# Masks a level ahead, one projection moved, norm sums two fills later, and weight slabs in 8 KB rows

## Time and profile before

| | |
|---|---|
| median of three runs | 1447.91 us |
| profiled execution: its own time | 1451.15 us |
| its span, first to last instruction | 1449.3 us |
| mean granted clock of TensorE | 0.926 |
| busy share PE / DVE / ACT / POOL | 80% / 51% / 34% / 26% |
| DMA: bytes, mean rate | 377.58 MB, 261 GB/s |
| chain that ended last | PE 48%, DMA 24%, DVE 18%, ACT 7% |

### The profile page before, as it was taken

How to read it: one execution, slowest core, us unless ns; L and a number is a source line. 1 busy time by engine, 2 the same in 40 slices (tenths; PEclk the granted TensorE clock), 3 DMA queues, 4 the chain that set the end, 5 groups by cost and what they waited for, 6 DMA issues and landing times.

```text
span 1449.3 us, 15054 instructions
## 1 busy us (share of the span) xinstructions
PE 1160.8 (80%) x5592; PEld 674.0 (47%) x5592; DVE 745.7 (51%) x1811; ACT 487.0 (34%) x1283; POOL 370.6 (26%) x285
## 2 busy tenths in 40 slices
PE   6799885868867676666677766679988998999997
PEld 2588653422422231111122221134866887889883
DVE  5113468758769965465444445530455656652102
ACT  1022124443433433344333333321576543112201
POOL 0868202243434444433343433300000000000000
PEclk9998998999988999998998999989998999999999
DMA  9953605789999999999999999915422131114230
GB/s 365 304 218 146 246 1 201 308 326 416 412 414 420 410 412 397 421 421 407 423 386 404 396 401 422 421 65 176 174 68 107 59 117 60 60 59 160 73 116 29
DMA packets 92164, 377.58 MB, mean 261 GB/s; under 512 B 6355, under 2 KB 9596, under 8 KB 59260
## 3 DMA queue, kind: packets, MB, share of 16 engines
q0 software_dynamic: 36864, 268.45, 45.3%
q1 hardware_dynamic: 54560, 106.13, 20.4%
q10 hardware_dynamic: 668, 2.04, 0.4%
HBM read 375.54 MB, written 1.06 MB: 260 GB/s over the span
## 4 chain that ended last, share of the span: by engine, by line
PE 48%; DMA 24%; DVE 18%; ACT 7%; issue 2%; POOL 1%; SPq 1%; DVEq 0%; POOLq 0%; ACTq 0%
PE ps L87 48%; DMA AR<-in_puv,idx 20%; DVE AR L87 8%; DVE RT L87 3%; ACT L87 2%; DVE tok L87 2%; DMA mixT<-scr 1%; ACT av L87 1%; DMA W<-in_w_mod 1%; DVE acc L87 1%; DVE rowb L87 1%; DVE mixT L87 1%; ACT acc L87 1%; POOL AR L87 1%; ACT rowb L87 1%
## 5 line engine op out<-in xcount | busy, mean ns | idle before, releaser
L87 PE MATMUL ps<-AR,acc 128*64 128x512 f32 x960 | 371.2, 689 | 184.3 <-ACT acc L87 183.1
L87 POOL DMA_INDIRECT AR<-in_puv,idx x256 | 278.1, 1086 | 502.1 <-PE ps L87 394.0
L87 PE MATMUL ps<-hT,W 128*128 128x256 f32 (+2 forms) x1504 | 324.6, 374 | 2.6 <-ACT hT L87 2.5
L87 PEld LDWEIGHTS ps<-hT,W 128*128 128x128 f32 (+1 forms) x1504 | 270.4, 195 | 54.8 <-issue 15.9
L87 PEld LDWEIGHTS ps<-AR,acc 128*64 128x64 f32 x960 | 90.2, 149 | 439.3 <-ACT acc L87 356.8
L87 DVE CUSTOM_DVE_ANT_0 AR<-AR,mixT 128x1024 f32<-128x1024 f32 x128 | 156.7, 1227 | 157.0 <-DMA AR<-in_puv,idx 156.8
L87 DVE CUSTOM_DVE_ANT_0 AR<-AR,tok 128x1024 f32<-128x1024 f32 x128 | 153.1, 1219 | 66.3 <-DMA AR<-in_puv,idx 66.2
L87 ACT ACTIVATE av<-av 128x1 f32<-128x1 f32 x256 | 51.3, 200 | 311.5 <-DVE av L87 311.3
L87 ACT ACT_TABLE_LOAD x105 | 134.7, 1283 | 11.4 <-DVE tok L87 9.5
L87 PE MATMUL ps<-W,hT 128*128 128x512 f32 (+3 forms) x288 | 97.8, 497 | 0.8 <-ACT hT L87 0.8
L87 ACT ACTIVATE acc<-fold,av 128x64 f32<-128x64 f32 x240 | 83.5, 348 | 7.8
(11 more groups left out here) (230 smaller groups left out, 1087.5 us busy)
## 6 DMA issues: line engine op xcount, KB each, us to landing
W<-in_w_in SPq DMA_DIRECT2D x25, 2048.0 KB, 8.4
W<-in_w_mod SPq DMA_DIRECT2D x12, 2048.0 KB, 17.4
W<-in_w_out SPq DMA_DIRECT2D x2, 2048.0 KB, 10.3
W<-in_wq SPq DMA_DIRECT2D x2, 2048.0 KB, 10.2
AR<-in_puv,idx POOLq DMA_INDIRECT x256, 11.3
W<-in_wba SPq DMA_DIRECT2D x2, 2048.0 KB, 7.7
W<-in_wbb SPq DMA_DIRECT2D x2, 2048.0 KB, 8.6
W<-in_wo SPq DMA_DIRECT2D x2, 2048.0 KB, 7.7
```

Source lines behind the costliest of these rows:

```text
L87: ins = f(*args, **kw)
```

## The change

Four edits. In `load_w` a slab is read by two DMAs of 1 MB each, and the host lays every weight matrix out so that the eight pieces of a partition stand side by side in device memory: each DMA has 128 rows of 8 KB (of four times the slab's width where it is narrower than 512; then the rows in SBUF stay apart). The l2 norm's steps stand 0, 2, 3, 4 and 5 fills behind instead of 0 to 4. `za_step(3)` is issued after the first group's mask and difference, in front of its transposes. The masks of level 1 wait only for the difference, and those of level l + 1 are issued in level l, behind its first products, each after the last product that read its `CT[:, n]`.

```diff
             if i < len(plan):
                 src, a, n = plan[i]
-                landed[i] = SP.dma(nc.sync.dma_start, wsem[i % NSLOT], W[:, i % NSLOT, :, 0:n],
-                                   src[:, a:a + n].rearrange("(k p) n -> p k n", p=P), after=after)
+                for k in (0, 4):
+                    landed[i] = SP.dma(nc.sync.dma_start, wsem[i % NSLOT], W[:, i % NSLOT, k:k + 4, 0:n],
+                                       src[:, 8 * a + k * n:8 * a + (k + 4) * n].rearrange("p (k n) -> p k n", k=4), after=after)
...
-            for n, f in enumerate((l2_square, l2_sums, l2_diag, l2_spread, l2_scale)):
+            for n, f in ((0, l2_square), (2, l2_sums), (3, l2_diag), (4, l2_spread), (5, l2_scale)):
                 if s - n in L2:
                     f(L2.index(s - n))
...
-                za_step(n)
+                if n < 3:
+                    za_step(n)
...
             t = V(tt_, tt4, ident.unsqueeze(1).to_broadcast([P, 4, P]), CT[:, n], SUB,
                   after=[t, t_turn["q", 0], t_turn["q", 1]])
+            if n == 0:
+                za_step(3)
...
+        def masked(l, n, after):
+            return V(tt_, CT[:, n], MTv[n // 2][:, 4 * (n % 2):4 * (n % 2) + 4, :], mask(l), MUL, after=after)
+
+        t_cm = [masked(1, n, state[n][:1]) for n in range(4)]
+        t_xp = [None] * 4
         for l in range(1, 7):
             xs = []
             for n in range(4):
-                a, g4 = n // 2, n % 2
-                t = V(tt_, CT[:, n], MTv[a][:, 4 * g4:4 * g4 + 4, :], mask(l), MUL, after=state[n])
-                b, src, p_ = product(l, CT[:, n], Tm[:, 4 * n:4 * n + 4, :], [t] + state[n])
+                b, src, p_ = product(l, CT[:, n], Tm[:, 4 * n:4 * n + 4, :], [t_cm[n]] + state[n])
+                t_xp[n] = p_
...
+            if l < 6:
+                t_cm = [masked(l + 1, n, [t_xp[n]]) for n in range(4)]
             run_filler()
...
+    def slabs(w, cuts=None):
+
+        cuts = cuts or range(0, w.shape[1] + 1, 512)
+        return np.concatenate([w[:, lo:hi].reshape(8, P, hi - lo).transpose(1, 0, 2).reshape(P, -1)
+                               for lo, hi in itertools.pairwise(cuts)], axis=1)
```

More of the change, by code:

```diff
@@ L1 @@
+import itertools
 import math
@@ L1924 @@
     w_out = np.concatenate([pair(w_out[0:512]), w_out[512:]])
+    def slabs(w, cuts=None):
+        cuts = cuts or range(0, w.shape[1] + 1, 512)
+        return np.concatenate([w[:, lo:hi].reshape(8, P, hi - lo).transpose(1, 0, 2).reshape(P, -1)
+                               for lo, hi in itertools.pairwise(cuts)], axis=1)
     ins = [("x", a["x"][0]), ("cst", k), ("oh", onehot), ("pc", pc), ("cmpw", cmpw), ("keysT", keysT),
-           ("rel", a["rel_table"]), ("rows", rows), ("ab", ab), ("w_mod", a["w_mod"][0]), ("w_in", w_in),
-           ("w_out", w_out), ("wq", a["peer_wq"][0]), ("puv", np.concatenate([a["peer_u"][0], a["peer_v"][0]], axis=1)),
-           ("w_in2", a["w_in_2"][0]), ("wba", a["w_branch_a_2"][0]), ("wbb", a["w_branch_b_2"][0]),
-           ("wo2", a["w_out_2"][0])]
+           ("rel", a["rel_table"]), ("rows", rows), ("ab", ab), ("w_mod", slabs(a["w_mod"][0])),
+           ("w_in", slabs(w_in, (0, 512, 1024, 1304, 1816, 2328, 2840))),
+           ("w_out", slabs(w_out)), ("wq", slabs(a["peer_wq"][0])),
+           ("puv", np.concatenate([a["peer_u"][0], a["peer_v"][0]], axis=1)),
+           ("w_in2", slabs(a["w_in_2"][0], (*range(0, 8193, 512), 8208, 8720, 9232, 9744, 10256))),
+           ("wba", slabs(a["w_branch_a_2"][0])), ("wbb", slabs(a["w_branch_b_2"][0])), ("wo2", slabs(a["w_out_2"][0]))]
     nc = bacc.Bacc("TRN2", target_bir_lowering=False, num_devices=1)
```

## The result

The changed kernel took 1430.93 us (median of four runs, 1426.61 to 1434.69) against 1448.8 of the kernel before (four runs): a ratio of 0.9881 [0.9856, 0.9907]. Run again beside others it took 1430.29, a ratio of 0.9901 [0.9865, 0.9937]. Forecast were 1424 and the range 1411 to 1438. The time lies in that range, and about 18 us were gained instead of 24.

A forecast was written before the change was run, and what follows sets the result against it. The bound changes by stage: DMA gathers from 553 to 950 us, PE from 1128.2 to 1161.8. Gains 2.5 + 2 + 9.5 + 3 + 7 = 24 us, from the median 1447.9 to 1424; range 1411 to 1438.

The forecast's parts named there:

- rival A: Whole kernel: all gains come as summed, 1424 us, own range 1413 to 1433; chance 0.62.
- the start: Kernel start: X, K and `scr` come 5 us later, covered by PE's wait for `mixT`; `flip_bias` starts 2.5 us earlier.
- za: Last za projection: first transposes follow it at once, removing PE's 4.04 us idle; gain 3 us, bounds 1.5 and 4.
- the masks: Levels: masks fall into V's idle, so PE's five waits before levels 2 to 6 go; gain 7.0 us, bounds 5 and 7.5.
- the norm sums: Conv blocks: sums two fills behind spare PE the wait for the square; gain 9.5 us, bounds 3 and 13.
- rival C: Conv blocks: PE waits for diagonals instead, lower clock stays; norm change gains 3, not 9.5: 1430.5 us; chance 0.13.
- Gathers and the projection behind them: Gather stage: six slabs sharing DMA engines with the gathers give time back; gain 2 us, bounds 0 and 3.6.
- one more sum and one more spread: Norm steps after the seven columns, where PE is the bound: these fall there and cost 1.7 us together.
- The cover of 6.79 us: Start: PE's earlier wait for `mixT`, 6.79 us, which was to hide the later q projection.
- if PE also loses its half clock in these 6.18 us: Start: upper bound if `flip_bias`, then 6.18 us, no longer runs at half clock; gain 4 to 5 us.
- Rival D: Slab loads: long direct rows come slowly, slower than before, about 1510 or 1465 us; chance 0.07.
- Its second case: Slab loads: only w_mod's rows run at half rate because of their pitch, +5.6 us per slab; about 1465 us.

## Why the prediction was right, and where its sum was off

The forecast was faster, by the mechanisms of rival A, and faster it is: the start, za and the masks by the mechanisms that were forecast, the norm sums only in part. The time itself, 1430.9, is the number of rival C (1430.5). Its reason, PE waiting for diagonals, is not what came (0.4 us), but a part of its outcome is: waits that stay, and the lower clock behind them. That the number agrees is chance: C had 3 for the norm sums and all other terms as summed, and the ledger has 5.2, and terms that differ from the sum by up to 4.5. The terms, in us of the profiled pair: the start to `mixT` and what follows, forecast 2.5, measured 3.5 by the projection behind `flip_bias`. Gathers and the projection behind them, forecast 2, measured -2.5 (what was 3.5 ahead at 62 us is 0.98 at the first conv copy). Norm sums, forecast 9.5, measured 5.2. za, forecast 3, measured 2.5. Masks, forecast 7, measured 6.4 in the levels and 1.4 behind the last one: 7.8. In all 24 and 16.5.

**The failed step** is the norm sums' price. The column spacings were forecast as 5.6, 6.8, 4.7, 7.7, 4.7, 8.4 and 4.7, and came as 5.5, 6.6, 4.7, 7.5, 4.7, 11.7 and 4.7. All but one were right. The one is the column with the scale, and behind the seven another one with a scale took 9.6 us where 4.1 stood before (11.2 to 11.3 in four other kernels with the same norm steps, whose conv stages take 128.6 to 128.9 us); "one more sum and one more spread" and a wait "for a diagonal" had been priced there at 4.1 together, and 5.5 were lost. The prediction looked for the next wait at the diagonal and bounded it by a wait in each pair; rival C was the same thought. It was the PSUM bank of the spread, held until the scale, which the change also moves and which the prediction counted only as V's time. The two waits of 2.5 us stood in the list of PE's waits of the kernel before, for the very stretch of the earlier trace rows, and had not been read: the prediction put ACT's two idles of 3.47 us down to the square, and so expected them to go with it. With the scale moved, the stage gains 12.1 us (132.64 to 120.52), so the forecast size was available, though not by the edit that was forecast.

**The gather stage** was missed in the execution that the ledger uses, and met on average. From PE's first transposes of `rowb` (`K,rowb`) near 247 us to PE's transposes behind the last gather, the five kernels with 2 KB rows took 699.5 to 702.7 us (mean 700.9); seven others with 8 KB rows 695.6 to 699.3, and the changed kernel's own profile 701.7. The mean of all eight is 698.2: a gain of 2.7 where 2 had been said. The profile that the ledger uses is the worst of the eight, so the miss of 4.5 in this term says little of the edit. What differs from one execution to the next in that stage stays open, and no run tests whether the price of a row is what the average gains.

**What was right by its steps.** X lands 4.0 us later (V starts on it at 15.34 for 11.35), K 5.8 (16.9 us from issue to landing for 11.1) and `scr` 6.3; they had been forecast as 5, from one row for one row. The cover of 6.79 us held with little to spare, since the q projection starts 6.0 later and not 4.2: `flip_bias` starts 0.9 us earlier instead of 2.5. The bound "if PE also loses its half clock in these 6.18 us" made up for it, with 3.60 us: in all kernels with the longer rows it took 3.60 to 3.70 us, in those with 2 KB rows 5.27 to 6.73. That the start still gained more than the sum's 2.5 is due to this bound, which the sum had left out.

Rival D is refuted in both forms: direct rows of 8 and of 16 KB run at 26 GB/s per engine, and 11.8 belongs to something else in that load, which no run here isolates. The Trainium skill, page "DMA: Bandwidth & Descriptors", section "Latency and other measured facts", has copies slow down at row pitches of 512 KiB and more; w_mod's rows at 192 KiB ran at the full 26.1, which the rule as stated (it gives no figure below 512 KiB) does not contradict. Its second case in the prediction extended the rule to a pitch it does not name.

**The test that was set.** Slabs in 5 us: yes. `scr` near 19: 20.5. `mixT` no longer in front of PE: yes. Sums without idle on PE: for the square, yes, but the sums at 1118.48 wait 1.92 us for the bank; raw copies 43 us apart over seven columns: 45.5. No idle of 4 us behind za: 2.39 in its place, on the second group. No waits for `AR` before the levels: none.

## What to carry to other kernels

When a step is moved away from a wait, look at every buffer that the moved steps hold, above all a PSUM bank whose reader now stands behind more work of its engine; here the list of waits of the stretch before the change named the next one. When DMA rows are lengthened, look at what shares the engines in the other queue and how much cover stands behind its lateness: in these runs the two queues finished as many rows one as the other, whether a row was of 2, 8 or 16 KB. Read a stage's gain from several executions where PE's clock or the gathers are in play, and add by stages rather than by the times of single edits.

## What the runs showed of the hardware

- Two queues with work finished as many rows one as the other, with slab rows of 2, 8 and 16 KB (187 to 186 packets, 151 to 146, 98 to 104). ACT's queue moved 0.76 MB in 2.8 us, 0.60 MB in 4 us and 0.18 MB in 4 us beside them.
- A direct row of 8 KB or 16 KB moves at 26 GB/s per engine, one of 2 KB at 23: 16 KB gained nothing over 8 KB.
- SP's issues of the first four slabs took 14.65 us in rows of 2 KB, and 4.20 us as eight DMAs of 8 KB rows.
- The granted clock of one and the same column was 0.72 in one execution and 1.00 in another, 12.30 and 8.94 us, though PE's 36 matmuls and its 2.5 us of idle were alike in both.
